# Modulation weights in blocks of 512 columns: one contiguous stretch per partition and piece

## The chip, the cores and the metric

The kernel runs on one core of a Trainium2 chip. A core has TensorE (matrix products), VectorE, ScalarE and GpSimd, the queue engine SyncE, and 16 DMA engines that all queues share. The metric is device time in microseconds.

## The reference, cut to what matters

One block of a diffusion transformer (width D = 2048, 256 tokens and 256 context tokens, all float32): a modulation vector is computed from `c` and shifts, scales and gates everything behind it. `w_mod` has 2048 rows and 6 x 2048 columns, 100.7 MB.

```python
mod_x = (jax.nn.silu(c) @ w_mod[l] + b_mod[l])[:, None, :]
mod_c = (jax.nn.silu(c_ctx) @ w_mod[l] + b_mod[l])[None, None, :]
sh1x, sc1x, g1x, sh2x, sc2x, g2x = jnp.split(mod_x, N_MOD, axis=-1)
hx = rms_norm(x, norm_pre1[l]) * (1.0 + sc1x) + sh1x
hc = rms_norm(ctx, norm_pre1[l]) * (1.0 + sc1c) + sh1c
rw_x, z_x, xbc_x, dt_x, gate_x = jnp.split(hx @ w_in[l], IN_SPLITS, axis=-1)
...
x = x + g1x * rms_norm(mix_x, norm_post1[l])
h2x = rms_norm(x, norm_pre2[l]) * (1.0 + sc2x) + sh2x
x = x + g2x * rms_norm(peer_ffn(h2x, ...), norm_post2[l])
```

Between these lines stand an RWKV-7 branch, a Mamba-2 (SSD) branch and their merge; `peer_ffn` gathers expert rows.

## The kernel before

Each engine runs its own program, written out by hand; semaphores order them. The stages follow one another: front, RWKV, SSD, merge, experts. P = 128 partitions, KC = 16 chunks of 128 rows.

**The front stage** (`front`, lines 177 to 522). SyncE issues on its queue (q1 in the profile), in this order: the four row tiles of `ctx` and `x` (1 MB each, 8 KB per partition), the pieces 0 to 2 of `w_mod`, the first of four slices of `w_in` (`lora_weights(0)`, 128 x 4 runs of 2.5 KB, 1.3 MB), then pieces 3 to 6, slice 1, pieces 7 to 10, slice 2, and so on. A piece is 8 chunks by 512 columns, 2 MB, and goes to one of the three places of `ring`; `mod_piece(q)` waits from q = 3 on until piece q - 3 has been multiplied (`piece_mm`). The 16 pieces are the first 4096 columns, shift and scale.

ScalarE meanwhile issues on its own queue (q10) `ssm_d` and the parameter rows: 22 small loads of 2 to 128 rows of 512 bytes (line 338), into `raw`. One of them is 74 of the 96 rows of `b_mod`, near the end of the list. VectorE (line 383) and TensorE wait for all of them together (`raw_in`), because `c` is among the last.

TensorE transposes `raw` (line 462), ScalarE and VectorE make `silu_p` and `silu_c` from it, and TensorE multiplies pieces 0 and 1 (`row_piece`, line 472: 8 products of 128*32 by 512 in four column groups). Then it transposes the rows of x and ctx (line 498), runs `turn_row(0)` (line 481, after ScalarE has copied the row, line 353), pieces 2 and 3 and `turn_row(1)`. From there the four quarters follow:

```python
for b in range(QUARTERS):
    pe.wait_ge(w_in, 16 * (b + 1))
    if b < QUARTERS - 1:
        row_piece(4 * b + 4)
        for k in range(4):
            for n in range(6):
                low_rank(n, 4 * b + k)
            if k < 3:
                row_piece(4 * b + 5 + k)
```

`low_rank` (line 487) multiplies a slice of `w_in` with `hT`, which VectorE has scaled and shifted by the result of the pieces (line 441).

**The SSD stage** (`ssd`) reads the other 8192 columns, for `c` alone: 8 groups of 16 pieces of 2 chunks by 512 columns (512 KB) into the four places of `wm`. SyncE issues them (line 1409) as VectorE's products set places free; VectorE multiplies and adds (line 1603, 30 of 32 products of a group, two of them at another line). In the same stage ScalarE issues the `w_in` tiles (1 MB in 512-byte runs) four tiles ahead of TensorE, whose projections stand at line 1719.

Of the kernel before, what the change touches and what calls it, by code (L numbers as in the profile page):

```python
# [19 lines left out]
P = 128  # L20
D = 2048
KC = D // P
# [104 lines left out]
def hybrid_block(nc, a, out):  # L127
# [4 lines left out]
    with ExitStack() as whole:  # L132
# [4 lines left out]
        def sem(name):  # L137
# [26 lines left out]
        yaT = sb("yaT", [P, KC, SEQ])  # L164
        ybT = sb("ybT", [P, KC, SEQ])
        ssd(nc, sb, sem, ps, a, ident, ones, below, par, col, SKIP_D, silu_c, modT, hT, ybT, yaT, ya_out, ya_in, ya_dram,
            slots, w_tiles, ss_pe, dt_proj, ss_loads, mg_pe, mg_w, mg_first)
        tail(nc, sb, sem, ps, a, out, ident, ones, par, col, modT, hT, yaT, ybT, ya_in, slots, mg_pe, mg_w)
# [8 lines left out]
def front(nc, sb, sem, ps, a, rows, tiles, ident, ones, head_ones, head_mean, tri, below, par, col, silu_c, modT, hT,  # L177
# [3 lines left out]
    with ExitStack() as stage:  # L181
        def t(name, *shape):
# [27 lines left out]
        piece_in = [sem(f"mod_in{n}") for n in range(3)]  # L210
# [2 lines left out]
        w_in, proj, pads, padded, keeps, added, shifted, mus, funcs = (  # L213
            sem(x) for x in ("lora_w", "lora_proj", "lora_pads", "lora_padded", "lora_keeps", "lora_added", "lora_shifted",
                             "lora_mus", "lora_funcs"))
        w_mod = a["w_mod"].rearrange("l (k p) n -> (l p) k n", p=P)
        w_src = a["w_in"].rearrange("l (k p) n -> (l p) k n", p=P)
        QUARTERS = 4
        COLS = [c for b in range(QUARTERS) for c in (D + 512 * b, 512 * b)]
# [2 lines left out]
        for name, (at, ap, n, width) in rows.items():  # L222
            done = 0
            while done < n:
                tile, row = divmod(at + done, P)
                k = min(n - done, P - row)
# [3 lines left out]
        with nc.Block() as block:  # L230

            @block.sync
            def _(sp):
                def mod_piece(q):
                    if q >= 3:
                        sp.wait_ge(piece_mm, q - 2)
                    c0, k0 = COLS[q // 2], q % 2 * (KC // 2)
                    sp.dma_start(ring[:, q % 3, :].rearrange("p (k n) -> p k n", n=512),
                                 w_mod[:, k0:k0 + KC // 2, c0:c0 + 512]).then_inc(piece_in[q % 3], 16)

                def lora_weights(b):
                    sp.dma_start(w[:, 4 * b:4 * b + 4, :], w_src[:, 4 * b:4 * b + 4, L0:RW_COLS]).then_inc(w_in, 16)

                srcs = [a["ctx"], a["ctx"], a["x"], a["x"]]
                for n in range(NT):
                    lo = (n % 2) * P
                    sp.dma_start(x_rows[n], srcs[n][0, lo:lo + P, :]).then_inc(rows_in[n], 16)
                for q in range(3):
                    mod_piece(q)
                lora_weights(0)  # L250
                for b in range(QUARTERS):
                    for q in range(4 * b + 3, min(4 * b + 7, 16)):
                        mod_piece(q)
                    if b + 1 < QUARTERS:
                        lora_weights(b + 1)
                sp.wait_ge(turned, KC)
                first_weights(sp)
# [297 lines left out]
def rwkv(nc, sb, sem, ps, a, rows, tiles, ident, ones, head_ones, head_mean, tri, below, par, col, silu_c, modT, hT, ya_out, ya_dram,  # L555
# [10 lines left out]
    with ExitStack() as stage:  # L566
# [34 lines left out]
        def first_weights(sp):  # L601
# [3 lines left out]
            weights(sp, 0, 1)  # L605

        front(nc, sb, sem, ps, a, rows, tiles, ident, ones, head_ones, head_mean, tri, below, par, col, silu_c, modT, hT,
              per_pair, shifts, tanh_w, low_a, gate_g, (pad, em, ln_eps, off, strict, incl, neg2, id32, id64), first_weights, flat_slots)

# [732 lines left out]
def ssd(nc, sb, sem, ps, a, ident, ones, below, par, col, SKIP_D, silu_c, modT, hT, ybT, yaT, ya_out, ya_in, ya_dram,  # L1342
        slots, w, PA, proj, loads, PG, mg_w, first_in):

    with ExitStack() as stage:
# [9 lines left out]
        rows_sem, sums, dv, ac, per_done, heads_done = (  # L1355
            sem(x) for x in ("dt_rows", "dt_sums", "dt_dve", "dt_act", "dt_per_group", "dt_heads"))
        w_in = a["w_in"].rearrange("l (k p) n -> (l p) k n", p=P)
        w_mod = a["w_mod"].rearrange("l (k p) n -> (l p) k n", p=P)
        in_columns = lambda m: m.rearrange("p (r w) -> p w r", r=GRID_R)

        SLOTS_W, SLOTS_M = 4, 4
        WM, PADS = SLOTS_M * 2 * 512, 4 * 2 * (SEQ + 4)
        wm = slots[:, 1, 0:WM].rearrange("p (q m c) -> p q m c", q=SLOTS_M, m=2)
# [23 lines left out]
        mod_in, consts = [sem(f"ss_w_mod{n}") for n in range(SLOTS_M)], sem("ss_consts")  # L1387

        def tile(engine, m):
            if m < 6 * GROUPS:  # L1390
                c0 = column(m // 6, m % 6)
                engine.dma_start(w[m % SLOTS_W], w_in[:, :, c0:c0 + P]).then_inc(loads[m % SLOTS_W], 16)
# [5 lines left out]
        with nc.Block() as block:  # L1398

            @block.sync  # L1400
            def _(sp):
                def mod_piece(g, m):
                    q = g * KC + m
                    if q >= SLOTS_M:
                        m_last = 2 * (q - SLOTS_M) + 1
                        sp.wait_ge(*VM.by(f"m{m_last % (2 * KC)}", m_last // (2 * KC)))
                    b, k = divmod(2 * m, KC)
                    c0 = (MOD0 + g * MOD_PER) * P + b * 512
                    sp.dma_start(wm[:, q % SLOTS_M, :, :], w_mod[:, k:k + 2, c0:c0 + 512]).then_inc(mod_in[q % SLOTS_M], 16)

                sp.dma_start(dt_bias[:, :], a["ssm_dt_bias"].rearrange("l d h -> l (d h)").broadcast_to([P, 2 * SH])).then_inc(rows_sem, 16)
                sp.dma_start(a_exp[:, :], a["ssm_a_log"].rearrange("l d h -> l (d h)").broadcast_to([P, 2 * SH])).then_inc(rows_sem, 16)
                for n in range(2, SLOTS_W):
                    tile(sp, n)
                for n in range(2):
                    sp.wait_ge(ya_out[n], 8 * PAIRS)
                sp.dma_start(yaT[:, :, :], ya_dram).then_inc(ya_in, 16)
                for g in range(GROUPS):
                    for m in range(KC):
                        mod_piece(g, m)  # L1420
                for c in range(4):
                    sp.wait_ge(*PA.by(TILES[2 + c], GROUPS - 1))
                    sp.dma_start(w[c], w_in[:, :, GA0 + c * P:GA0 + (c + 1) * P]).then_inc(first_in[c], 16)
                sp.wait_ge(*VA.by("c3_4", GROUPS - 1))
                sp.wait_ge(*PB.by("mod", GROUPS - 1))
                sp.dma_start(slots[:, 1, :].rearrange("p (k n) -> p k n", n=512), w_in[:, :, GA0 + D:GA0 + D + 512]).then_inc(mg_w[1], 16)
# [1097 lines left out]
```

## Time and profile before

| | |
|---|---|
| median of 3 runs | 4236.61 us (4233.58 to 4238.69) |
| the profiled execution, its own time | 4234.48 us |
| its span | 4232.7 us |
| TensorE busy | 3804.2 us (90%) |
| VectorE busy | 2031.0 us (48%) |
| DMA | 872.93 MB, mean 206 GB/s |
| pieces of `w_mod` | 16 of 2 MB, 128 of 512 KB |

All times in rows are counted from the start of the span. In a timeline row the first number is the start, the second the duration; rows of one kind that follow each other are merged (x32), and the bracket tells how long the engine was idle before and what ended that. PE is TensorE, DVE is VectorE, ACT is ScalarE, SPq and ACTq are the issuing of DMAs on SyncE's and ScalarE's queue. A matmul in float32 stands in the records as two instructions and more, so that a piece of 8 products is x16 or x32. PEclk 1.00 is 2.4 GHz, 0.50 is 1.2 GHz. A DMA share of over 1 means that packets of one engine overlap.

### The profile page before, as it was taken

How to read it: one execution, taken by the hardware profiler on the slowest of the kernel's cores; microseconds unless marked ns; L12 is line 12 of the kernel's file. 1: busy time of each engine (PE TensorE's matmuls, PEld its weight loads, DVE VectorE, ACT ScalarE, POOL GpSimd, SP SyncE). 2: the span in 40 equal slices, each digit the busy share in tenths (PEclk: the TensorE clock that was granted, in tenths of full speed). 3: DMA queues.
4: the chain of work that ended last, by engine and by line, in shares of the span. 5: the costliest groups of instructions: out<-in, count | busy, mean ns of one | idle time of the engine just before them, and what ended most of it. 6: DMA issues, size and time to landing. Idle time of an engine off the chain costs nothing. (4 is left out here: it accounts for less than half of the span.)

```text
span 4232.7 us, 81256 instructions
## 1 busy us (share of the span) xinstructions
PE 3804.2 (90%) x35655; PEld 2313.7 (55%) x35655; DVE 2031.0 (48%) x3409; ACT 729.5 (17%) x1318; POOL 778.2 (18%) x755
## 2 busy tenths in 40 slices
PE   7999999999999989999999999988777777777777
PEld 3466666666666655666668888565223223322323
DVE  1355565556555547767770000035554554554541
ACT  2223222322233212221220000010110111111101
POOL 3000000001000100000010000004544444444431
PEclk9999999999999989999999999999999999999999
DMA  9211111111111117655663444437999999999996
GB/s 380 86 35 49 47 49 37 48 47 41 45 46 42 32 30 246 201 172 184 199 194 140 159 159 172 171 135 309 406 402 428 405 408 428 406 408 427 407 427 243
DMA packets 408824, 872.93 MB, mean 206 GB/s; under 512 B 16556, under 2 KB 250686, under 8 KB 341310
## 3 DMA queue, kind: packets, MB, share of 16 engines
q0 software_dynamic: 73728, 536.90, 30.5%
q1 hardware_dynamic: 243072, 284.82, 19.8%
q10 hardware_dynamic: 91710, 46.43, 3.8%
q8 instruction: 269, 4.41, 0.4%
q14 instruction: 45, 0.37, 0.0%
HBM read 863.87 MB, written 4.23 MB: 205 GB/s over the span
## 5 line engine op out<-in xcount | busy, mean ns | idle before, releaser
L2482 PE MATMUL ps<-w_slots,diag 128*128 128x512 f32 x2048 | 970.7, 622 | 302.6 <-DMA w_slots<-in_peer_v,ixv 264.5
L2482 PEld LDWEIGHTS ps<-w_slots,diag 128*128 128x128 f32 x2048 | 385.6, 197 | 887.5 <-issue 555.3
L979 PE MATMUL ps<-hT,w_slots 128*128 128x512 f32 (+1 forms) x1536 | 636.1, 542 | 3.1 <-PEq L230 2.2
L1719 PE MATMUL ps<-hT,w_slots 128*128 128x256 f32 (+1 forms) x1504 | 500.3, 486 | 6.5 <-PEq L655 4.9
L2334 DVE SCALAR_TENSOR_TENSOR junk<-w_slots,hT 128x2048 f32<-128x2048 f32 x128 | 293.4, 2292 | 290.3 <-DMA w_slots<-in_peer_u,ixu 289.6
L2334 DVE SCALAR_TENSOR_TENSOR junk<-ybT,hT 128x2048 f32<-128x2048 f32 x128 | 293.5, 2293 | 268.1 <-DMA ybT<-in_peer_u,ixu 266.3
L2237 POOL DMA_INDIRECT w_slots<-in_peer_v,ixv x256 | 293.7, 1147 | 550.0 <-PE ps L2482 497.3
L1719 PEld LDWEIGHTS ps<-hT,w_slots 128*128 128x128 f32 x1504 | 281.8, 191 | 173.3 <-issue 152.7
L979 PEld LDWEIGHTS ps<-hT,w_slots 128*128 128x128 f32 x1536 | 269.1, 191 | 179.7 <-issue 156.0
L2401 ACT ACTIVATE diag<-ident,coef 128x128 f32<-128x128 f32 x256 | 101.0, 400 | 1000.3 <-PE ps L2482 990.1
L695 POOL TENSOR_TENSOR bonus<-Kh 128x256 f32<-128x256 f32 x16 | 11.8, 735 | 1185.3 <-DVE Kh L916 1185.3
L2229 POOL DMA_INDIRECT ybT<-in_peer_u,ixu x128 | 170.1, 1329 | 196.2 <-PE ps L2482 81.5
L1603 DVE SCALAR_TENSOR_TENSOR w_slots<-w_slots,silu_c 128x512 f32<-128x512 f32 x240 | 193.9, 808 | 13.4 <-DVE w_slots L1603 0.9
L824 DVE SCALAR_TENSOR_TENSOR w_slots<-ps,em,w_slots 128x64 f32<-128x64 f32 x448 | 106.2, 278 | 195.0 <-PE ps L1078 195.0
L1986 PE MATMUL ps<-hT,w_slots 128*128 128x256 f32 x896 | 194.1, 379 | 0.3 <-PEq L1398 0.3
L1986 PEld LDWEIGHTS ps<-hT,w_slots 128*128 128x128 f32 x896 | 170.2, 190 | 23.8 <-issue 0.7
L844 DVE TENSOR_TENSOR w_slots<-ps,off 128x1024 f32<-128x1024 f32 x128 | 150.5, 1217 | 51.9 <-PE ps L1053 51.9
L2124 DVE TENSOR_TENSOR sga<-sga,ps 128x1024 f32<-128x1024 f32 x4 | 4.9, 1221 | 298.7 <-PE ps L1986 298.7
L2229 POOL DMA_INDIRECT w_slots<-in_peer_u,ixu x128 | 138.3, 1081 | 52.1 <-issue 42.7
L1078 PEld LDWEIGHTS ps<-w_slots 64*64 64x64 f32 x1792 | 71.1, 135 | 127.2 <-issue 109.4
L2448 PE MATMUL ps<-h2T,w_slots 128*128 128x256 f32 x512 | 115.7, 388 | 9.6 <-DMA w_slots<-in_peer_wq 8.4
L1439 POOL TENSOR_TENSOR xw<-xt,heads 128x256 f32<-128x256 f32 x48 | 27.7, 612 | 478.0 <-ACT xt L1498 478.0
(381 smaller groups left out, 4683.7 us busy)
## 6 DMA issues: line engine op xcount, KB each, us to landing
w_slots<-in_w_mod SPq DMA_DIRECT2D x128, 512.0 KB, 4.8
w_slots<-in_w_in SPq DMA_DIRECT2D x56, 1024.0 KB, 5.8
w_slots<-in_w_in ACTq DMA_DIRECT2D x44, 1024.0 KB, 6.9
w_mod_ring<-in_w_mod SPq DMA_DIRECT2D x16, 2048.0 KB, 12.6
w_slots<-in_w_in SPq DMA_DIRECT2D x7, 4096.0 KB, 13.8
w_slots<-in_w_branch_a SPq DMA_DIRECT2D x4, 4096.0 KB, 13.8
w_slots<-in_w_branch_b SPq DMA_DIRECT2D x4, 4096.0 KB, 13.8
w_slots<-in_w_out SPq DMA_DIRECT2D x4, 4096.0 KB, 12.7
```

Source lines behind the costliest of these rows:

```text
L824: stt(state(d, c), ps[:, 6, d * HEAD:(d + 1) * HEAD], em[:, z % 2, d, c:c + 1], state(d, c), ALU.mult, ALU.add).then_inc(*VD.did(f"c{j}_{d}"))
L844: tt(F[:, 2 * d:2 * d + 2, :, :], ps[:, 0:4, d * SEQ:(d + 1) * SEQ].rearrange("p r (h c) -> p h r c", h=2), off[:, l - 1, d, :].unsqueeze( ...
L979: last = mm(ps[:, 4, t0:TOK], w[m % 2][:, k, :], hT[:, k, t0:TOK], start=(k == 0), stop=(k == KC - 1))
L1603: stt(by_row[:, b, :], part, silu_c[:, k, 0:1], by_row[:, b, :], ALU.mult, ALU.add).then_inc(*VM.did(f"m{m}"))
L1719: last = mm(out, w[m % SLOTS_W][:, k, :], hT[:, k, t0:TOK], start=(k == 0), stop=(k == KC - 1))
L1986: last = mm(ps[:, bank + c // 2, (c % 2) * SEQ:(c % 2 + 1) * SEQ], slot[n][:, k, c * P:(c + 1) * P], rhs[:, k, :], start=(k == 0), stop=(k ...
L2229: nc.gpsimd.indirect_dma_start(ub[b], None, u_tab, bass.IndirectOffsetOnAxis(ap=ixu[:, n, k:k + 1], axis=0)).then_inc(u_in[b], 16)
L2237: nc.gpsimd.indirect_dma_start(vb[b], None, v_tab, bass.IndirectOffsetOnAxis(ap=ixv[:, n, k:k + 1], axis=0)).then_inc(v_in[b], 16)
L2334: nc.vector.scalar_tensor_tensor(junk[:, :], ub[k % NB], 1.0, h2_rows[:, n, :], ALU.mult, ALU.mult, accum_out=dots[:, k:k + 1]).then_inc(* ...
L2401: nc.scalar.activation(diag[:, k % 2, :], ident[:, :], ACT.Copy, scale=coef[:, k:k + 1]).then_inc(*DG.did(f"dg{k}"))
L2448: last = nc.tensor.matmul(ps[:, h % 2, s * SEQ:(s + 1) * SEQ], wq_at[h % 2][:, k, s * P:(s + 1) * P], h2T[:, k, :], start=(k == 0), stop=( ...
L2482: last = nc.tensor.matmul(ps[:, 4 * n + c, :], diag[:, k % 2, :], vb[k % NB][:, c * 512:(c + 1) * 512], start=False, stop=False)
```

## The change

The host hands `w_mod` over as an array of 24 blocks of 512 columns, [block, partition, chunk, 512]. What one partition reads of a front piece is one stretch of 8 x 512 floats (16 KB), where it was eight of 2 KB; of an SSD piece one stretch of 4 KB, where it was two of 2 KB. The stretches of neighbouring partitions start 32 KB apart; before, rows started 48 KB apart. The values that reach the chip's memory buffers, their places, the instructions and the waits are the same. The layout on the host is not part of the time.

```diff
@@ front
-        w_mod = a["w_mod"].rearrange("l (k p) n -> (l p) k n", p=P)
+        w_mod = a["w_mod"].rearrange("m p k n -> p m k n")
@@ front, mod_piece
                     sp.dma_start(ring[:, q % 3, :].rearrange("p (k n) -> p k n", n=512),
-                                 w_mod[:, k0:k0 + KC // 2, c0:c0 + 512]).then_inc(piece_in[q % 3], 16)
+                                 w_mod[:, c0 // 512, k0:k0 + KC // 2, :]).then_inc(piece_in[q % 3], 16)
@@ ssd
-        w_mod = a["w_mod"].rearrange("l (k p) n -> (l p) k n", p=P)
+        w_mod = a["w_mod"].rearrange("m p k n -> p m k n")
@@ ssd, mod_piece
-                    sp.dma_start(wm[:, q % SLOTS_M, :, :], w_mod[:, k:k + 2, c0:c0 + 512]).then_inc(mod_in[q % SLOTS_M], 16)
+                    sp.dma_start(wm[:, q % SLOTS_M, :, :], w_mod[:, c0 // 512, k:k + 2, :]).then_inc(mod_in[q % SLOTS_M], 16)
@@ kernel
+    laid = dict(inputs)
+    laid["w_mod"] = np.asarray(inputs["w_mod"]).reshape(KC, P, -1, 512).transpose(2, 1, 0, 3)
     for name in _NAMES:
-        v = np.ascontiguousarray(inputs[name])
+        v = np.ascontiguousarray(laid[name])
```

## Rows read from the trace of the kernel before

**Rows 1.** The page: busy times, DMA share and GB/s, chain that ended last.

```profile
PE 3804.2 (90%) x35655; PEld 2313.7 (55%) x35655; DVE 2031.0 (48%) x3409; ACT 729.5 (17%) x1318; POOL 778.2 (18%) x755
...
DMA  9211111111111117655663444437999999999996
GB/s 380 86 35 49 47 49 37 48 47 41 45 46 42 32 30 246 201 172 184 199 194 140 159 159 172 171 135 309 406 402 428 405 408 428 406 408 427 407 427 243
...
DMA 20%; PE 8%; issue 3%; DVE 3%; POOL 0%; DVEq 0%; ACT 0%; POOLq 0%; ACTq 0%
```

**Rows 2.** The page's costliest groups and its DMA issues.

```profile
L1719 PE MATMUL ps<-hT,w_slots 128*128 128x256 f32 (+1 forms) x1504 | 500.3, 486 | 6.5 <-PEq L655 4.9
...
w_slots<-in_w_mod SPq DMA_DIRECT2D x128, 512.0 KB, 4.8
...
w_mod_ring<-in_w_mod SPq DMA_DIRECT2D x16, 2048.0 KB, 12.6
```

**Rows 3.** Line 1603, the products with the pieces in the SSD stage: its waits.

```profile
  DMA w_slots<-in_w_mod: 0.8, 1
```

**Rows 4.** TensorE's waits from 0 to 70 us: total, times, longest.

```profile
PE ps L472 <- DMA w_mod_ring<-in_w_mod: 2.4, 1, 2.4
```

**Rows 5.** Timeline from 0 to 126 us: start, duration, instruction, idle before it.

```profile
11.47 0.44 ACTq L338 DMA_DIRECT2D raw<-in_c_ctx  x1
...
16.88 5.73 SPq L242 DMA_DIRECT2D w_slots<-in_w_in  x1
...
21.63 0.31 DVE L383 COPY raw<-skip 16x64 f32<-16x64 f32 x2 [21.63 <-DMA raw<-in_c_ctx]
...
25.04 4.94 PE L472 MATMUL ps<-w_mod_ring,w_slots 128*32 128x512 f32 x32 [1.43 <-DVE w_slots L394]
...
43.09 1.05 PE L481 MATMUL ps<-pick,w_slots 128*128 128x2 f32 x8 [0.72 <-ACT w_slots L353]
...
46.56 3.64 PE L472 MATMUL ps<-w_mod_ring,w_slots 128*32 128x512 f32 x16 [2.42 <-DMA w_mod_ring<-in_w_mod]
50.13 5.25 PE L487 MATMUL ps<-hT,w_slots 128*96 128x512 f32 x12
...
88.61 1.92 PE L472 MATMUL ps<-w_mod_ring,w_slots 128*32 128x512 f32 x16
...
97.67 4.54 PE L487 MATMUL ps<-hT,w_slots 128*96 128x512 f32 x12
...
115.57 1.92 PE L472 MATMUL ps<-w_mod_ring,w_slots 128*32 128x512 f32 x16
```

**Rows 6.** Window by engines: busy, granted clock (PEclk), DMA share, GB/s.

```profile
70.00:85.00 15.00, 15.00 (x74) 6.26 (x67) 2.84 (x9) 1.19 (x2) 0.00 (x0) 1.00 1.05 395
```

**Rows 7.** Half-microsecond windows around the fall of the clock, same columns.

```profile
44.50:45.00 0.50, 0.00 (x0) 0.00 (x0) 0.50 (x2) 0.00 (x0) 0.42 (x2) 0.79 1.02 377
...
51.50:52.00 0.50, 0.50 (x2) 0.16 (x1) 0.00 (x0) 0.00 (x0) 0.43 (x2) 0.89 1.05 385
```

**Rows 8.** DMA queues from 7.5 to 9.5 us: packets, MB, share of 16 engines.

```profile
q1 hardware_dynamic: 116, 0.82, 98.5%
q10 hardware_dynamic: 110, 0.03, 6.6%
```

**Rows 9.** DMA queues from 13.5 to 15.5 us.

```profile
q1 hardware_dynamic: 296, 0.61, 87.0%
q10 hardware_dynamic: 267, 0.11, 20.6%
```

**Rows 10.** DMA queues from 17.5 to 19.5 us.

```profile
q1 hardware_dynamic: 370, 0.73, 102.5%
q10 hardware_dynamic: 34, 0.02, 3.3%
```

**Rows 11.** DMA queues from 11.5 to 13.5 us.

```profile
q1 hardware_dynamic: 152, 0.70, 87.8%
```

**Rows 12.** DMA issues from 0 to 26 us: size, us from issue to landing.

```profile
w_slots<-in_w_in SPq DMA_DIRECT2D x1, 1280.0 KB, 18.1
```

## The prediction

> **What bounds the kernel now.** I read the page first. One core, TensorE busy for 90% of the span, the DMA engines full only in the first slices and in the last third, where the expert rows are gathered, and the chain of work that ended last names only that last third [rows 1]. The modulation weights are read in two places: 16 pieces of 2 MB in the front stage and 128 pieces of 512 KB in the SSD stage [rows 2]. So two stages can change, and each was read for what ends its waits.
>
> SSD stage: TensorE's 1504 projection products there sat idle before them for only 6.5 us in all, 4.9 of it for TensorE's own sequencer, once, at the start of the stage [rows 2]. The VectorE products that read the pieces waited once for one, for 0.8 us [rows 3]. A transfer there is cover, not path.
>
> Front stage: up to 70 us TensorE has waited only once for a weight piece, for 2.4 us [rows 4]. The timeline shows the order: the last parameter load lands at 21.63 us, the first product with a piece starts at 25.04, the second `turn_row` runs 43.09 to 44.14, and piece 4 starts at 46.56, after the 2.42 us wait [rows 5]. From there TensorE has no gap: the second piece of the second quarter starts at 88.61 and that of the third at 115.57, one quarter in 26.96 us, with the same durations each time [rows 5]. A quarter needs 4 pieces and one slice of `w_in`, 8.39 + 1.31 = 9.70 MB, or 360 GB/s over 26.96 us. DMA moves 395 there, at a share of 1.05 [rows 6]. It is full because it catches up; nobody waits for it. So from 46.56 us on TensorE sets the time, and the chain before it is: parameter rows, then 19.1 us of TensorE and ScalarE work (25.04 to 44.14), then piece 4.
>
> **The change, part by part.**
>
> *Bytes and instructions.* No instruction is added or removed. A front piece goes from 128 x 8 runs of 2 KB to 128 runs of 16 KB; an SSD piece from 256 runs of 2 KB to 128 of 4 KB.
>
> *The transfer itself.* 2 KB runs move at about 390 GB/s (395 in this window [rows 6]), 5.4 us for a piece. The nearest row for long runs is the gather of 8 KB rows, 428 GB/s [rows 1], 4.9 us. Bound below: no gain. I take 0.5 us a piece, as the 16 KB run is beyond the 8 KB one.
>
> *What that buys.* By piece 4 five pieces have passed: 5 x 0.5 = 2.4 us, which just covers the only wait, 2.42 us. After it TensorE is the bound, so more is not to be had. While TensorE waited, its granted clock fell from 2.4 to 1.2 GHz, from about 44.8 to 51.6 us [rows 7]: piece 4 took 3.64 us instead of the 1.92 of the later ones, and the projections behind it 5.25 instead of 4.54 [rows 5], together 2.43 us. The fall begins 0.7 us into the wait, so with no wait I take it as gone; at worst it stays. The gain is 2.4 to 4.85 us, and it cannot be more.
>
> *SSD stage.* Nothing: 0.8 us of waiting at most can go [rows 3]. The `w_in` tiles on ScalarE's queue share the engines with the pieces. At most four slots, 2 MB, can stand ahead of a tile, as before, and a tile is asked for four tiles ahead of its use; this lead is the cover, and TensorE's products, back to back, show it [rows 2]. Without it a piece ahead of a tile would cost 512 KB at 390 GB/s, 1.3 us. I take zero.
>
> *What stands beside the pieces.* This is the step I think decides. The parameter rows are 23 small loads, issued by ScalarE on queue q10, the last at 11.5 us [rows 5], as 512-byte packets. SyncE's queue q1 holds x and ctx (8 KB packets), pieces 0 to 2 and the first `w_in` slice. They share the same engines. In windows of 2 us, packets of q1 against q10: 116 to 110 while q1 carries 8 KB, 296 to 267 while it carries 2 KB [rows 8, 9]. The engines alternate packet for packet, whatever the packets weigh. In bytes the share is 0.82 to 0.03 MB in the first and 0.61 to 0.11 in the second. So the small loads speed up when x is through and 2 KB packets come. After the change 16 KB packets come instead, eight times as long.
>
> The tail: from 17.5 us q10 has 34 packets in 2 us while q1 has 370, 23 per engine [rows 10]. That fits alternation on two of the 16 engines: 17 packets each, one per 0.118 us. Such a straggler load is the 74-row part of `b_mod`.
> By the Trainium skill (DMA: Bandwidth & Descriptors, the section on why a DMA increments its semaphore by 16) a load runs on the largest number of engines up to 16 that divides its rows, for 74 rows two, 37 packets each; the rows of the trace agree.
>
> How many packets such an engine still has when x ends, at about 13 us (in the window 11.5 to 13.5 q1's 152 packets are 0.70 MB, a mixture of both sizes [rows 11]): the load lands at 21.63, some 0.8 us after its last packet, so (20.8 - 13.0)/0.118 = 66. On the same engine q1 will then hold 3 x 8 packets of 16 KB, 32 of the `w_in` slice, and 4 for completions: 60. 66 against 60, one for one: the last parameter row goes out when q1 is empty, no earlier. When is that? SyncE issues nothing more before piece 0 is multiplied, and this waits for the parameters. Before, the first `w_in` slice, the last in that backlog, is issued at 16.88 and lands 18.1 us later, at 35.0 [rows 5, 12]. With three pieces 0.5 us shorter each: 33.5 us, and the six packets left over are 0.2 us.
>
> So the parameters land at about 33.5 us instead of 21.63: **+11.9 us** for all that hangs on them, which is `silu`, then pieces 0 and 1, the transposes, everything in the 19.1 us. Bound below: 0, if the engines shared by bytes. Bound above: 13.4 us, if the backlog gains nothing from long runs. Had the straggler 10 packets fewer, it would end four places before the end of the `w_in` slice, at about 0.13 us for a place: 11.2 us. Pieces 3 and 4 are then issued at 39 and 42 us into an idle queue and are there long before 55; the 2.42 us wait goes by this alone.
>
> **Sum**, against the profiled execution (4234.48 us, of which the span is 4232.7): +11.9 for the parameters, -2.42 for the wait, -2.43 for the clock, 0 for the SSD stage = +7.0 us, 4241.5. Behind the front stage all stages are in a row and only shift. The median of the three runs is 2.1 us above the profiled one: 4236.6 + 7.0 = **4243.6 us**.
>
> **Rivals.**
>
> 1. *The clock still falls.* `turn_row` at 43.09 is preceded by 0.7 us of waiting for ScalarE and has only 128x2 products, so TensorE does little for 1.8 us even without the wait for piece 4. For: before, the fall comes right after. Against: it came in the added idle time, and in the later quarters `turn_row` comes at full clock [rows 6]. Then +9.4 us, 4246.0, slower by 0.22%. It decides once the parameters land after 32.5 us.
>
> 2. *The long packets don't hold up the small ones*: the engines take turns by bytes, or the 16 KB run is served in parts. Against it the counts at two sizes [rows 8, 9]. For: no row shows 16 KB packets beside small ones. Then the parameters land at 21.6 or sooner, and only the gain stays: -2.4 to -4.85 us, 4231.8 to 4234.2.
>
> 3. *The runs are not joined*: still 2 KB packets, nothing changes, 4236.6. Against: source and destination of a piece are now both contiguous per partition.
>
> 4. *The new addresses are slow.* A partition's run now starts 32 KB behind its neighbour's, a power of two, where it was 48 KB. If a piece took twice as long, 10.8 us, a quarter would need 4 x 10.8 + 3.4 = 46.6 us of DMA against 27 of TensorE, and the front stage would be bound by DMA: some 60 us more over three quarters, about 4300. It decides from 5.9 us a piece on. For it no row; the gather reads rows 8 KB apart at 428 GB/s [rows 1]. The Trainium skill (DMA: Bandwidth & Descriptors, latency and other measured facts) warns of row pitches at large powers of two, with 207 GB/s at 512 KiB, nearly full, and 103 at 4 MiB; by it 32 KB would cost nothing. No run here shows it.
>
> **How the numbers follow.** Alternation holds and the parameters land late: 0.76, of which the clock stays up 0.46 (my forecast) and falls 0.30 (rival 1). Rival 2: 0.14. Rival 3: 0.05. Rival 4: 0.03. Others, such as code loading behind long packets: 0.02. A measurement of this kernel can tell about 0.2%, 8.5 us, from no change; slower by that is above 4245.1. Of the forecast's 0.46 about 0.08 ends above it, of rival 1 about 0.2, rival 4 and the others 0.05: slower 0.33. Faster by 0.2% would need more than the largest gain found: 0.03. Same: 0.64. The range runs from the middle of rival 2, 4232.5, to rival 1 with the parameters a us later and the scatter of the runs, 4249. The likeliest one's own range is 4240 to 4247.
>
> **What the profile after would show.** DMA packets fewer by 16 x 896 + 128 x 128 = 30,720. VectorE's copy of `skip` into `raw`, which waits for all parameter rows, at about 33.5 us instead of 21.63; at 21.6 rival 2 is right. TensorE's first piece at 36.9. In 2 us windows before that, q1 and q10 with about equal counts, but only some 50 packets each. No wait of TensorE for a piece, no clock of 0.5 between 50 and 62 us. A quarter still 26.96 us; longer means rival 4. The SSD stage as long as before. The prediction is wrong if the first piece is where it was, or if a stage behind the front changes its length.

## The result, and the profile after

The change makes the kernel slower by 0.21%: over 17 runs each the median is 4241.42 us against 4233.04 before, ratio 1.0021 with a 95% interval of 1.0013 to 1.0029. In us of before that is +8.9 (5.5 to 12.3): small, but clear of the noise. A second series on another chip gave 1.0022 (1.0013 to 1.0030).

The page of the changed kernel: span, busy times, packets and the queue that carries the pieces.

```profile
span 4232.9 us, 81256 instructions
...
PE 3786.4 (89%) x35655; PEld 2306.4 (54%) x35655; DVE 2030.7 (48%) x3409; ACT 731.0 (17%) x1318; POOL 773.6 (18%) x755
...
DMA packets 378104, 872.93 MB, mean 206 GB/s; under 512 B 16556, under 2 KB 250686, under 8 KB 308542
...
q1 hardware_dynamic: 212352, 284.82, 19.4%
```

The packets are 30,720 fewer than 408,824, exactly what 16 KB and 4 KB runs make, so the runs were joined and rival 3 is out. The span of this one execution is that of before. A single execution scatters more than the difference (4230 to 4250 us), so the place of the loss is read in the front stage, and its size from the timed series.

The front stage, engines merged (start, duration, instruction, idle before it), answers to [rows 5]:

```profile
2.93 1.51 SPq L238 DMA_DIRECT2D w_mod_ring<-in_w_mod  x3
...
4.48 0.51 SPq L242 DMA_DIRECT2D w_slots<-in_w_in  x1
...
34.15 0.28 DVE L383 COPY raw<-skip 16x64 f32<-16x64 f32 x2 [34.15 <-DMA raw<-in_c_ctx]
...
37.62 0.20 PEld L472 LDWEIGHTS ps<-w_mod_ring,w_slots 128*32 128x32 f32 x8 [1.93 <-DVE w_slots L394]
...
41.32 15.03 SPq L238 DMA_DIRECT2D w_mod_ring<-in_w_mod  x4
```

SyncE now has its whole backlog issued by 5 us: the first `w_in` slice is issued at 4.48 us, not at 16.88. The parameters have landed at 34.15 us instead of 21.63, and the first product with a piece starts at 37.62 instead of 25.04. Only at 41.32 does SyncE issue piece 3. In between the DMA engines move nothing from about 33 us to 42 us, as the windows show (engines as in [rows 6], DMA share and GB/s last):

```profile
36.00:37.00 1.00, 0.09 (x1) 0.00 (x0) 0.72 (x2) 0.25 (x2) 0.86 (x3) 1.00 0.00 0
...
41.00:42.00 1.00, 1.00 (x12) 0.31 (x8) 1.00 (x2) 0.00 (x0) 0.92 (x2) 1.00 0.00 0
...
57.00:58.00 1.00, 1.00 (x11) 0.81 (x14) 0.19 (x2) 0.00 (x0) 0.85 (x3) 1.00 1.03 426
...
61.00:62.00 1.00, 1.00 (x4) 0.38 (x3) 0.00 (x0) 0.00 (x0) 0.00 (x0) 1.00 1.00 426
```

The first two windows, at 36 and at 41 us, move nothing; before, DMA moved 393 and 387 GB/s in the same windows. In the last one, at 61 us, pieces move at 426 GB/s: 4.9 us for one, as estimated. The clock is 1.00 all the way.

TensorE alone, from the transposes on:

```profile
44.14 0.44 PE L498 MATMUL ps<-ident,w_slots 128*128 128x128 f32 x2 [0.34 <-DVE in_rows L398]
...
56.68 1.05 PE L481 MATMUL ps<-pick,w_slots 128*128 128x2 f32 x8 [0.72 <-ACT w_slots L353]
57.67 1.92 PE L472 MATMUL ps<-w_mod_ring,w_slots 128*32 128x512 f32 x16
59.52 4.54 PE L487 MATMUL ps<-hT,w_slots 128*96 128x512 f32 x12
63.99 1.92 PE L472 MATMUL ps<-w_mod_ring,w_slots 128*32 128x512 f32 x16
...
97.28 1.92 PE L472 MATMUL ps<-w_mod_ring,w_slots 128*32 128x512 f32 x16
```

`turn_row` at 56.68 was at 43.09. Piece 4 follows it at once, at 57.67; it was at 46.56, so the 2.42 us wait is gone. It takes 1.92 us, not 3.64, and the projections 4.54, not 5.25: the clock did not fall. The second piece of the second quarter is at 97.28, +8.67 to before's 88.61. TensorE's waits in the front stage of the changed kernel (total, times, longest). Left out are 1.5 us for `silu_p` ahead of the first piece, which were 1.43 before, and 2.2 us at the end of the stage, which before has too:

```profile
PE ps L462 <- DVE raw L383: 34.6, 1, 34.6
...
PE ps L487 <- DVE hT L441: 1.1, 1, 1.1
PE ps L481 <- ACT w_slots L353: 0.7, 1, 0.7
PE ps L498 <- DVE in_rows L398: 0.3, 1, 0.3
```

No piece among them. The SSD stage is as it was, products with the pieces and their wait:

```profile
L1603 DVE SCALAR_TENSOR_TENSOR w_slots<-w_slots,silu_c x240: 740/751/2730, 1608.1 to 2195.9; 128x512 f32<-128x512 f32 x120
...
  DMA w_slots<-in_w_mod: 0.9, 1
```

The queues' packets in two windows, to be held against [rows 9]. From 13.5 to 15.5 us:

```profile
q1 hardware_dynamic: 48, 0.79, 97.5%
q10 hardware_dynamic: 48, 0.01, 3.0%
```

and from 25.5 to 27.5 us:

```profile
q1 hardware_dynamic: 54, 0.88, 104.5%
q10 hardware_dynamic: 36, 0.01, 2.2%
```

48 to 48, where it was 296 to 267: each small packet now pays for a 16 KB one. Later q10's count drops below q1's, which fits that only some engines have small packets left. At the end of the loads, from 32.5 to 33.5 us, q1 has 7 packets left and q10 24.

### The profile page after: what moved, and what is told of

Read it like the earlier page. It is cut to its first block and busy times, and to the rows that moved or that the text cites. A ratio compares the mean times of both kernels' runs of the same rounds, so it can differ in the third digit from the quotient of the medians.

```text
span 4232.9 us, 81256 instructions
## 1 busy us (share of the span) xinstructions
PE 3786.4 (89%) x35655; PEld 2306.4 (54%) x35655; DVE 2030.7 (48%) x3409; ACT 731.0 (17%) x1318; POOL 773.6 (18%) x755
## 5 line engine op out<-in xcount | busy, mean ns | idle before, releaser
L1603 DVE SCALAR_TENSOR_TENSOR w_slots<-w_slots,silu_c 128x512 f32<-128x512 f32 x240 | 193.9, 808 | 13.5 <-DMA w_slots<-in_w_mod 0.9
L2448 PE MATMUL ps<-h2T,w_slots 128*128 128x256 f32 x512 | 115.8, 389 | 12.8 <-DMA w_slots<-in_peer_wq 11.5
```

What stands on the lines that cost most here:

```text
L1603: stt(by_row[:, b, :], part, silu_c[:, k, 0:1], by_row[:, b, :], ALU.mult, ALU.add).then_inc(*VM.did(f"m{m}"))
L2448: last = nc.tensor.matmul(ps[:, h % 2, s * SEQ:(s + 1) * SEQ], wq_at[h % 2][:, k, s * P:(s + 1) * P], h2T[:, k, :], start=(k == 0), stop=( ...
```

## The experiments

All ratios are to before, measured beside it on the same chip. The time of the copy into `raw` is that at which the parameters have landed. The RWKV stage starts when the front stage is done, so its start tells what the front stage gained or lost in the profiled execution.

| kernel | copy into raw, us | piece 4 starts, us | RWKV stage starts, us | median, us | ratio (95%) |
|---|---|---|---|---|---|
| before | 21.63 | 46.56 | 150.65 | 4228.56 to 4233.04 in four series | 1 |
| after | 34.15 | 57.67 | 159.31 | 4241.42 | 1.0021 (1.0013 to 1.0029) |
| front_only | 34.15 | 57.66 | 159.30 | 4239.97 | 1.0023 (1.0011 to 1.0034) |
| ssd_only | 21.81 | 46.31 | 149.62 | 4228.77 | 0.9997 (0.9985 to 1.0009) |
| hold | 16.06 | 47.59 | 150.89 | 4232.79 | 1.0006 (0.9996 to 1.0017) |
| split_rows | 30.56 | 53.76 | 155.41 | 4234.40 | 1.0012 (1.0002 to 1.0022) |
| run4k | 26.55 | 50.20 | 151.85 | 4233.45, one run | |
| run8k | 32.77 | 55.94 | 157.59 | 4234.73, one run | |
| before_split | 18.01 | 46.41 | 149.70 | 4233.54 | 0.9996 (0.9983 to 1.0009) |
| slice_first | 34.54 | 58.27 | 159.92 | 4239.10, one run | |
| slice_first_split | 21.27 | 44.06 | 147.36 | 4226.93 | 0.9992 (0.9980 to 1.0004) |
| slice_first_split2 | 21.01 | 43.81 | 145.46 | 4224.73 | 0.9989 (0.9979 to 1.0000) |
| after_again | 34.26 | 57.81 | 159.46 | 4237.80 | 1.0022 (1.0013 to 1.0030) |

The two columns agree: against before the RWKV stage starts 8.7 us later in after and front_only, 4.8 in split_rows, 0.2 in hold, 1.0 earlier in ssd_only and in before_split, 3.3 and 5.2 earlier in the two runs of slice_first_split. The ratios are, in us and in this order, +8.9, +9.7, +5.1, +2.5, -1.3, -1.7, -3.4 and -4.7, each uncertain by 3 to 6. What a kernel gains or loses in the front stage is what it gains or loses in all, within that.

**One stage at a time: front_only and ssd_only.** The weights are handed over in both layouts, and one stage reads the old one.

```diff
# front_only, in ssd:
-        w_mod = a["w_mod"].rearrange("m p k n -> p m k n")
+        w_mod = a["w_mod_rows"].rearrange("l (k p) n -> (l p) k n", p=P)
...
-w_mod[:, c0 // 512, k:k + 2, :]
+w_mod[:, k:k + 2, c0:c0 + 512]
# ssd_only: the same two edits in front
```

> Blocks in the front stage alone; the SSD stage reads the old layout (a second copy of the weights is handed over for it). Theory, small loads held up beside 16 KB packets: all of the change's loss is here. The copy into raw starts at 34.2 us (+-0.5), as after the change, and the time is 6 to 11 us above before (ratio 1.0015 to 1.0026). Rival, the loss is in the SSD stage or spread over the kernel: ratio below 1.001 although the parameters are as late.

> Blocks in the SSD stage alone; the front stage as before. Theory: nothing changes, ratio 0.9995 to 1.0005, the copy into raw at 21.6 us, the first piece product at 25.0. Rival, 4 KB packets hold up ScalarE's w_in tiles: ratio 1.001 or more and a TensorE wait for w_slots in the SSD stage.

The whole loss is in the front stage: 1.0023, and the copy into `raw` at 34.15 us, to the hundredth as after the change. In the SSD stage the change does nothing that can be measured, 0.9997.

**The pieces held back: hold.**

```diff
+                sp.wait_ge(raw_in, 16 * (len(pieces) + 1))
                 for q in range(3):
                     mod_piece(q)
```

> After, but SyncE waits for all parameter loads before it issues the first piece. Theory: the small loads share the engines with the 8 KB rows of x and ctx alone, then have them alone: the copy into raw at about 16 us. The first piece then lands at about 23 us; the first product stays at about 25 us, as ScalarE's squares come before its sigmoid. Piece 4 lands at about 47 us, so the wait of TensorE for it is back, and the whole is as before: ratio to before 0.999 to 1.0005, that is 8 us less than after. Rival, long runs cost time in themselves: it stays at after's time (ratio 1.002).

The parameters land at 16.06 us. TensorE's products with pieces:

```profile
23.46 3.64 PE L473 MATMUL ps<-w_mod_ring,w_slots 128*32 128x512 f32 x16 [5.45 <-DMA w_mod_ring<-in_w_mod]
28.27 1.92 PE L473 MATMUL ps<-w_mod_ring,w_slots 128*32 128x512 f32 x16 [1.17 <-DMA w_mod_ring<-in_w_mod]
...
42.49 1.92 PE L473 MATMUL ps<-w_mod_ring,w_slots 128*32 128x512 f32 x16 [2.27 <-DMA w_mod_ring<-in_w_mod]
...
47.59 3.41 PE L473 MATMUL ps<-w_mod_ring,w_slots 128*32 128x512 f32 x13 [1.41 <-DMA w_mod_ring<-in_w_mod]
```

(The view ends within piece 4, so that it counts 13 of its 16 instructions; the whole takes 3.51 us.) Four waits for pieces, 10.3 us in all, since DMA starts them at 16 us. Yet piece 4 starts only a us later than before, and the ratio is 1.0006, an interval that holds 1 and lies mostly below after's 1.0021. With the same long runs the loss is gone once the small loads don't stand beside them; that long runs cost anything in themselves is not seen. The first product came at 23.46, earlier than the 25 I expected: ScalarE's sigmoid was free at 22.4.

**The size of the runs: run4k and run8k.** The host puts 64 bytes behind every 4 KB (8 KB) of a front piece, so that runs of this size can't be joined. The SSD stage reads the old layout in both.

```diff
+    laid["w_mod"] = np.pad(laid["w_mod"].reshape(-1, P, KC // 2, 2 * 512), ((0, 0), (0, 0), (0, 0), (0, 16)))
...
-w_mod[:, c0 // 512, k0:k0 + KC // 2, :]
+w_mod[:, c0 // 512, k0 // 2:(k0 + KC // 2) // 2, 0:2 * 512]
```

> Front pieces in runs of 4 KB (64 bytes of padding behind each run keep them apart), the SSD stage as before. Theory, the engines alternate packet for packet: a pair of a 4 KB packet and a small one takes about 0.18 us, 66 pairs from 13 us on: the copy into raw at 26 to 27 us. Rival, only packets above some size hold up others: 21.6 us. Rival, any change of the layout does it: 34 us.

> Front pieces in runs of 8 KB, kept apart in the same way, the SSD stage as before. Theory, packet for packet: 48 pairs of 0.33 us and then 18 of 0.13 us: the copy into raw at 32 to 33.5 us, little sooner than with 16 KB, as the backlog of SyncE's queue ends it in both. Rival, by bytes: 21.6 us. Rival, delay in proportion to the run: half way between 21.6 and 34.2, at 28.

run4k, the copy and the two queues from 13.5 to 15.5 us:

```profile
26.55 0.42 DVE L383 COPY raw<-skip 16x64 f32<-16x64 f32 x2 [26.55 <-DMA raw<-in_c_ctx]
```

```profile
q1 hardware_dynamic: 174, 0.71, 91.2%
q10 hardware_dynamic: 173, 0.07, 13.5%
```

run8k, the same:

```profile
32.77 0.41 DVE L383 COPY raw<-skip 16x64 f32<-16x64 f32 x2 [32.77 <-DMA raw<-in_c_ctx]
```

```profile
q1 hardware_dynamic: 95, 0.78, 97.5%
q10 hardware_dynamic: 93, 0.03, 6.8%
```

174 to 173, 95 to 93, 48 to 48 with 16 KB, and with the 2 KB of the old layout 287 to 287 in before_split (below), where no engine has run out of small packets yet: at four sizes of the long packet the counts are equal to a few packets. The landing grows with the size, 21.6, 26.6, 32.8 and 34.2 us, but not in proportion. In run8k SyncE's queue holds 48 packets of 8 KB, 32 of the slice and 4 for completions, 84 places, more than the 66 small packets that the prediction counts, so the parameters are in 1.4 us before the slice (issued at 4.51, landed at 34.2). With 16 KB there are only 60 places, so that the small packets outlast the queue; by this count a still longer run would hold them up no further, which no run tried. Both landings are inside what one for one gives, and neither fits a share by bytes. The padding also moves the starts of the runs off the pitch of 32 KB; as the landing follows the size of the runs all the same, the pitch is not what held the small loads up.

**The stragglers: split_rows.** In the list of parameter loads a load of more than 16 rows is cut to a multiple of 16 and a rest.

```diff
                 k = min(n - done, P - row)
+                if k > 16:
+                    k -= k % 16
```

> After, with the parameter loads whose row count isn't a multiple of 16 cut into a multiple of 16 and a rest (74 rows of b_mod become 64 and 10, 22 become 16 and 6, twice), three loads more. Theory, one for one and two engines with the most packets: the two engines lose some 33 packets, but 30 or so remain for each engine against 24 long ones, so the copy into raw comes at 31 to 32 us, only 2 to 3 us sooner than after's 34.15, and the time is 2 to 3 us below after's. Rival, the long load alone is the trouble: the copy at 22 us or less and the time of before or better.

The queues from 17.5 to 19.5 us:

```profile
q1 hardware_dynamic: 67, 0.84, 99.2%
q10 hardware_dynamic: 65, 0.03, 5.4%
```

67 to 65, so all engines still have small packets, and none is left with a tail of its own. The landing is at 30.56 us, 3.6 sooner (I had expected 2 to 3), the ratio 1.0012. The long load is part of the delay, the smaller one.

**Order and cut: slice_first, slice_first_split, before_split.**

```diff
# slice_first and slice_first_split
+                lora_weights(0)
                 for q in range(3):
                     mod_piece(q)
-                lora_weights(0)
# slice_first_split and before_split also have the cut of split_rows
```

> After, with only the order changed: the first w_in slice ahead of the three pieces, the parameter loads uncut. Theory, one for one and two engines that have 66 small packets left where x ends: 60 places of SyncE's queue go by in any order, so the order alone gains nothing: the copy into raw at 33.5 to 34.5 us. Rival, the order did it and the cut was not needed: 22 us or less.

> After, with the loads cut as in split_rows and the first w_in slice issued ahead of the three pieces, so that the rest of the small loads alternates with its 2.5 KB packets and not with 16 KB ones. Theory: the copy into raw at 22 to 24 us, the first piece product at 25.5 to 27.5, the second turn_row about 1 us after before's, no wait of TensorE for piece 4, clock up: 2 to 4 us below before, ratio 0.999 to 0.9995. Rival, pieces that come 4 us later are now waited for: piece 0 ends a wait of TensorE, and the time is before's or more.

> Before, with the loads cut as in split_rows and nothing else. Theory: the copy into raw comes at 19 to 20 us, but ScalarE's squares, now 1.4 us later behind three more loads, keep the sigmoid at 24 us or later, and piece 4 is waited for as before: ratio 0.9997 to 1.0003. Rival, the parameters' landing passes straight through to the end: 2 us below before.

slice_first, the copy:

```profile
34.54 0.42 DVE L383 COPY raw<-skip 16x64 f32<-16x64 f32 x2 [34.54 <-DMA raw<-in_c_ctx]
```

The order alone gains nothing, 34.54 us: 66 packets on the fullest engines outlast 60 places in whatever order these come. The cut and the order together let the small packets out beside those of 2.5 KB, and the landing is at 21.3 us. One part of what I expected of slice_first_split failed: piece 4 was waited for after all, 0.50 us, and its product took 3.08 us, so the clock fell. before_split says what the cut is worth without the change: the parameters land at 18.01 us, 3.6 sooner (a us before what I expected), the first product starts at 24.77, 0.3 us sooner, and the ratio is 0.9996. There ScalarE's squares end at 22.7 us and hold the sigmoid, which starts at 24.0.

**The better one, timed again: slice_first_split2, with after_again beside it.**

> The same kernel as slice_first_split, timed again, as its ratio of 0.9992 did not settle whether it beats before. Theory: front stage 3.3 us shorter than before's at the start of the RWKV stage, so 0.999 to 0.9995 again. Rival, no gain reaches the end: 1.0 or more.

> The changed kernel on the same chip as slice_first_split2. Theory: 6 to 11 us above before, 9 to 14 above slice_first_split2, the copy into raw at 34.2 us again. Rival, part of the loss belongs to one chip: a ratio to before under 1.001.

slice_first_split2, TensorE's first piece, second `turn_row` and piece 4:

```profile
24.85 4.98 PE L474 MATMUL ps<-w_mod_ring,w_slots 128*32 128x512 f32 x32 [1.90 <-DVE w_slots L396]
...
42.59 1.05 PE L483 MATMUL ps<-pick,w_slots 128*128 128x2 f32 x8 [0.72 <-ACT w_slots L355]
43.81 1.92 PE L474 MATMUL ps<-w_mod_ring,w_slots 128*32 128x512 f32 x16 [0.16 <-issue]
```

Piece 4 follows `turn_row` almost at once, at full clock; it is the same kernel as slice_first_split, so this small wait comes and goes between executions, and 1.9 us of front stage with it (145.46 against 147.36 us). The medians are 4226.93 and 4224.73 us against 4231.49 and 4228.56 of before beside them, 4.6 and 3.8 us less, and on one chip 13.1 us less than the change as it was made. Each interval against before ends at or just above 1: that it beats after is shown, that it beats before by a tenth of a per cent is likely, and no more.

## Why the prediction was right

**The step that decides held, and nearly its size.** Small loads and pieces alternate packet for packet; the parameters land when SyncE's backlog is empty. Predicted 33.5 us, measured 34.15. The end of the backlog was right, the slice lands at 33.4 us. What was short was the rest behind it: I had six packets left over, 0.2 us, and did not add them; the 24 of q10 after 32.5 us are about twelve on each of two engines, and the copy comes 0.75 us behind the slice. The first product was to come at 36.9 and came at 37.62. That the small packets on two engines slightly outnumber the places agrees with three more runs: the order alone changes nothing (slice_first), the cut brings the landing to 30.6, and with hold it is at 16.1. The prediction's side case of ten packets fewer, 11.2 us, is a slip by its own terms: four places of 0.13 us less than 11.9 are 11.4. Nothing else uses it.

**The wait and the clock.** The 2.42 us wait went, by the late start alone. The clock stayed up where it had fallen, at 1.00 through all windows from 36 to 62 us: the likelier of the two by a narrow margin, 0.46 against 0.30. Rival 1 is out. It is no luck of one execution. In the eight profiles where piece 4 wasn't waited for (after, after_again, front_only, split_rows, run4k, run8k, slice_first, slice_first_split2) the product with it takes 1.92 or 1.93 us; in those where it was waited for, 0.5 to 2.4 us long (before, ssd_only, hold, slice_first_split, before_split), 2.55 to 3.64 us.

**The transfer.** 426 GB/s, 4.9 us a piece, as taken from the gather. Rival 4 had asked for over 5.9 us. The Trainium skill (DMA: Bandwidth & Descriptors, latency and other measured facts) gives 207 GB/s at a row pitch of 512 KiB and 103 at 4 MiB, for copies between tensors in HBM; it has no figure for 32 KB, where this trace shows no loss. A quarter still takes 26.96 us (97.28 to 124.24). Rival 2 fell with the counts of 48 to 48.

**The SSD stage.** Nothing, as said; its wait went from 0.8 to 0.9 us, and ssd_only is at 0.9997.

**The sum was 1.7 us short.** At the front stage's end it should have been +7.0. Measured there:

```profile
159.31 8.82 PE L979 MATMUL ps<-hT,w_slots 128*128 128x512 f32 x20 [2.16 <-PEq L230]
167.97 1.06 PE L990 MATMUL ps<-lw,tanh_w 97*128 97x128 f32 x8
```

before, the same two:

```profile
150.65 10.49 PE L979 MATMUL ps<-hT,w_slots 128*128 128x512 f32 x20 [2.16 <-PEq L230]
160.97 1.06 PE L990 MATMUL ps<-lw,tanh_w 97*128 97x128 f32 x8
```

The RWKV stage starts at 159.31 instead of 150.65, +8.66 us. The terms: +12.52 for the landing (I had 11.9), +0.06 to the first product, +1.25 that I did not have (below), -0.24 up to the second `turn_row`, -2.48 for the wait and -2.44 for the clock, which makes +8.67. The median moved by 8.4 us and the ratio says 8.9 (5.5 to 12.3), so the front stage accounts for it. That the second line is only 7.0 us later comes from before's clock, which was 0.50 from 152 to 154 us: the 20 products took 10.49 us instead of 8.82. This fall also shows up in before_split, run4k and run8k and not in the nine others, ssd_only with the same front stage as before among them; it is scatter.

The level of the forecast was helped by luck. It stood on a median of three runs, 4236.6; over 17 runs before is at 4233.0. So the 4243.6 us were 3.6 too high by their base and 1.4 too low by the change (7.0, where the medians moved by 8.4), which together leaves them only 2.2 off. The prediction also said that a measurement can tell no less than 0.2%; the series of 17 tells 0.21% from nothing, with an interval of 0.08% to either side.

The missed 1.25 us: with the start moved, VectorE scales the rows of x and ctx (four products of 128x2048) while GpSimd is at products of two tensors for its masks. After:

```profile
37.56 3.73 DVE L398 TENSOR_SCALAR w_slots<-w_slots,in_rstd 128x2048 f32<-128x2048 f32 x2
```

```profile
37.54 1.27 POOL L312 TENSOR_TENSOR tri<-tri,blocks 128x512 f32<-128x512 f32 x1
38.89 1.32 POOL L316 TENSOR_TENSOR off<-blocks 128x128 f32<-128x128 f32 x1
```

before, the same kinds of instructions, when they didn't meet (VectorE's stood beside GpSimd's memsets then):

```profile
24.97 2.54 DVE L398 TENSOR_SCALAR w_slots<-w_slots,in_rstd 128x2048 f32<-128x2048 f32 x2
```

```profile
43.28 0.45 POOL L316 TENSOR_TENSOR off<-blocks 128x128 f32<-128x128 f32 x1
```

The first two products take 3.73 us instead of 2.54, all four 6.52 us (37.56 to 44.08) instead of 5.28, and the transposes wait for the last (44.14 against 30.31, +13.83 where the first product is at +12.58). Most of it is in the first one alone: it took 2.33 us, the next three 1.47 or 1.48, where before's four took 1.27 to 1.62. TensorE was slower too, 6.19 us for pieces 0 and 1 instead of 4.94, but that did not decide: in front_only it was done with them in 5.45 us, then waited 1.07 us, and the transposes started at 44.15 all the same.

The prediction called it a sign of being wrong if a stage behind the front changes its length. In the profiled execution one does: its span is not longer than before's, and it gains the time back in the RWKV stage: the SSD stage's first product with a piece is at 1608.1 us (above), and before at

```profile
L1603 DVE SCALAR_TENSOR_TENSOR w_slots<-w_slots,silu_c x240: 743/751/2726, 1610.0 to 2197.9; 128x512 f32<-128x512 f32 x120
```

1610.0. The timed series don't show this gain, and after_again's span is 4237.2, front_only's 4244.8. It is scatter: from the first product of line 979 to the first of line 1603, work that none of the kernels changes, the thirteen profiles take 1447 to 1463 us, after 1448.8, before 1459.4 and after_again 1455.7. From there to the first product of the next stage it is 635.8 us in before and in after. Why the RWKV stage varies by 16 us between executions stays open.

## What to carry to other kernels

Long contiguous runs made a transfer faster (here 9%), and made it a worse neighbour. If small loads on another queue share the DMA engines with it and something waits for them, count packets, not bytes: what is left of the small ones on the fullest engine, against the packets queued beside them. Before the layout of a bulk transfer is changed, get the small loads that the first products need out of its way. Putting them ahead of it brought the time back to before's (hold). Spreading them evenly over the engines gained 3.6 of the 12.5 us (split_rows), putting them beside the transfer with the shorter packets nothing (slice_first), both together all of it (slice_first_split). And a transfer that nobody waits for gives nothing back when it gets faster.

## What the runs showed of the hardware that I had not expected

- The alternation is exact to a few packets in 2 us while all engines have small packets, from 2 KB to 16 KB: 287 to 287 (before_split), 174 to 173, 95 to 93, 48 to 48. The 296 to 267 of before is 29 apart, which fits engines that had run out.
- VectorE and GpSimd held each other up, and for the most part the one that came second paid. VectorE's product of 128x2048 by a column took 1.27 us at best. Started 0.02 us behind GpSimd's product of 128x512 it took 2.33, and in run4k, 0.03 us ahead of a memset of 128x1548, 2.49 (the pair below), while GpSimd's instructions kept the 1.27 and 1.39 us that they also take alone. In run8k VectorE's product started 0.33 us ahead, and GpSimd's product of 128x512 took 2.12 us. The short ones of GpSimd, 128x128, took 1.32 us instead of 0.45 beside VectorE's. So the kind of GpSimd's instruction is not what decides; that whoever is first keeps the other out is my reading of these rows, and run4k's product, which was first by 0.03 us, does not quite fit it.

```profile
30.11 3.68 DVE L398 TENSOR_SCALAR w_slots<-w_slots,in_rstd 128x2048 f32<-128x2048 f32 x2
```

- Issuing three pieces took SyncE 13.9 us with 1024 packets each, 6.1 with 512 each (run4k), and 1.5 us with 128 each. The slice behind them, 512 packets in every kernel, took 5.73 us to issue in before, 6.12 in run4k and 0.51 in after. So what was queued ahead held the issuing engine, and not the number of its own packets.
